# Suffix sums of the stick-breaking heads as two fp32r passes over a high and a low part, in place of one fp32 pass

## The reference

```
z = einsum('bqhd,bshd->bhqs', qb, k) * scale
past = key_pos[None, :] < qpos[:, None]
log_keep = where(past, log_sigmoid(-z), 0.0)
suffix = cumsum(log_keep, axis=3, reverse=True) - log_keep
w = where(past, exp(log_sigmoid(z) + suffix), 0.0)
o = einsum('bhqs,bshd->bqhd', w, v)
```

## Time and profile before

| | |
|---|---|
| median of 3 runs | 1950.08 us |
| lowest, highest | 1949.14, 1953.25 us |
| the profiled execution | 1951.19 us, span 1949.5 us |
| PE busy | 1723.2 us, 88% of the span |
| DVE busy | 1026.1 us, 53% |
| ACT busy | 653.0 us, 33% |
| POOL busy | 591.1 us, 30% |
| stick-breaking stage | about 608 to 730 us of the span |
| DSA stage | about 730 to 780 us of the span |

### The profile page before, as it was taken

The page is one execution under the profiler, slowest core; times in us unless marked ns, Lnnn a source line. Parts: engine busy times, 40 slices in busy tenths (PEclk is TensorE's granted clock), DMA queues, the critical chain, the costliest instruction groups (busy, mean ns, idle before and its releaser), DMA issues.

```text
span 1949.5 us, 23737 instructions
## 1 busy us (share of the span) xinstructions
PE 1723.2 (88%) x9380; PEld 1429.6 (73%) x9385; DVE 1026.1 (53%) x1305; ACT 653.0 (33%) x889; POOL 591.1 (30%) x515
## 2 busy tenths in 40 slices
PE   4997599788787789869999999899987799999997
PEld 3796489568786668748888787677766678888875
DVE  1568567575467675583333324655675743233344
ACT  4312255412122325243232212343444343332222
POOL 0005800262774000467887701222431300000012
PEclk8998799899788889989999999899997999999999
DMA  8553300143532000225565522221110222323221
GB/s 278 164 172 98 119 1 1 34 156 116 165 109 84 25 1 1 65 87 172 182 194 180 168 84 83 84 87 44 65 44 23 65 86 91 102 86 102 94 85 43
DMA packets 152521, 187.14 MB, mean 96 GB/s; under 512 B 6893, under 2 KB 117845, under 8 KB 152436
## 3 DMA queue, kind: packets, MB, share of 16 engines
q1 hardware_dynamic: 152436, 185.96, 29.6%
HBM read 183.85 MB, written 2.10 MB: 95 GB/s over the span
## 4 chain that ended last, share of the span: by engine, by line
PE 58%; POOL 16%; DVE 12%; issue 7%; ACT 4%; DMA 2%; POOLq 0%; SPq 0%; another core or an unknown queue 0%; DVEq 0%; ACTq 0%
PE ps L843 6%; PE ps L844 6%; PE ps L845 6%; POOL msum L627 5%; POOL mraw L620 5%; PE ps L1200 4%; PE ps L1201 4%; PE ps L1202 4%; PE ps L939 2%; PE ps L1234 2%; PE ps L863 2%; PE ps L1236 2%; PE ps L1235 2%; PE ps L865 2%; PE ps L866 2%
## 5 line engine op out<-in xcount | busy, mean ns | idle before, releaser
L1200 PE MATMUL ps<-uH,whi 128*128 128x512 f32 x704 | 278.6, 396 | 25.7 <-DVE uL L1841 25.4
L1202 PE MATMUL ps<-uH,wlo 128*128 128x512 f32 x704 | 276.5, 393 | 0.0
L1201 PE MATMUL ps<-uL,whi 128*128 128x512 f32 x704 | 276.1, 392 | 0.0
L1825 DVE TENSOR_TENSOR wlo<-wraw,whi 128x2048 fp32r<-128x2048 f32 x64 | 157.3, 2458 | 178.6 <-ACT whi L1372 178.4
L620 POOL TENSOR_TENSOR mraw<-mraw,cpad 128x1024 f32<-128x1024 f32 x64 | 129.1, 2017 | 380.8 <-PE ps L782 237.2
L1372 ACT ACTIVATE whi<-wraw 128x2048 fp32r<-128x2048 f32 x71 | 135.7, 1911 | 301.0 <-PE ps L845 268.0
L1200 PEld LDWEIGHTS ps<-uH,whi 128*128 128x128 f32 x704 | 133.7, 190 | 57.0 <-issue 20.8
L2344 DVE TENSOR_TENSOR wlo<-wraw,whi 128x2048 fp32r<-128x2048 f32 x22 | 51.2, 2327 | 206.8 <-ACT whi L1677 206.8
L1202 PEld LDWEIGHTS ps<-uH,wlo 128*128 128x128 f32 x704 | 133.4, 190 | 28.5
L1201 PEld LDWEIGHTS ps<-uL,whi 128*128 128x128 f32 x704 | 133.8, 190 | 27.4
L627 POOL TENSOR_TENSOR msum<-msum,mraw 128x512 f32<-128x512 f32 x96 | 150.8, 1571 | 7.5
(11 more groups left out here) (452 smaller groups left out, 3663.3 us busy)
## 6 DMA issues: line engine op xcount, KB each, us to landing
mraw<-in_w_mod_dram SPq DMA_DIRECT2D x104, 512.0 KB, 3.9
wraw<-in_w_gate_dram SPq DMA_DIRECT2D x22, 1024.0 KB, 5.3
wraw<-in_w_up_dram SPq DMA_DIRECT2D x22, 1024.0 KB, 5.5
wraw<-in_w_down_dram SPq DMA_DIRECT2D x16, 1024.0 KB, 5.0
wraw<-in_w_in_dram SPq DMA_DIRECT2D x11, 1024.0 KB, 5.5
wraw<-in_w_in_even_dram SPq DMA_DIRECT2D x9, 1024.0 KB, 6.6
mfirst<-in_w_mod_dram SPq DMA_DIRECT2D x16, 512.0 KB, 7.2
wraw<-in_w_in_odd_dram SPq DMA_DIRECT2D x16, 512.0 KB, 4.5
```

The lines of the kernel that those rows point to most:

```text
L1200: mm(o, h_, uH[:, k], start=(k == 0), stop=False)
L1201: mm(o, h_, uL[:, k], start=False, stop=False)
L1202: last = mm(o, l_, uH[:, k], start=False, stop=(k == KT - 1))
L1825: V.tensor_tensor(wlo[:, n % 2, :], wraw[:, n % 2, :], whi[:, n % 2, :].bitcast(F32), ALU.subtract).then_inc(lo_done, 1)
```

## The change

A head's softplus `spt` is split: ACT copies it to `spH` as fp32r (`sb_part`), DVE writes the rest `spt - spH` to `spL` as fp32r (`sb_rest`). PE's suffix sums become 10 fp32r matmuls over `spH` and 10 over `spL`, against fp32r copies `rtri` and `rone` of the two constant matrices, which ACT makes once. `spH` lies in the memory of `zw` and `spL` in that of `spt`, so `sb_min(h)` now waits for the suffix sums of head h-2 to be done. One top-k round stands ahead of the first `sb_rest`, and `dsa_max` and `dsa_move` get the width (q+1)*128.

```diff
             def sb_suffix(h):
-                z, s_ = region(h), spt[:, h % 2]
-                pe.wait_ge(sp_rd, h + 1)
-                for kt in range(4):
-                    for k2 in range(kt, 4):
-                        w = SEQ - k2 * P
-                        o0 = ZOFF[kt] + (k2 - kt) * P
-                        last = mm(z[:, o0:o0 + w], negtri[:] if k2 == kt else negone[:], s_[:, ZOFF[k2]:ZOFF[k2] + w],
-                                  start=False, stop=True, skip_group_check=True)
+                z = region(h)
+                if h == 0:
+                    pe.wait_ge(tri_rd, 1)
+                for part in range(2):
+                    s_ = (spH, spL)[part][:, h % 2]
+                    pe.wait_ge((sph_rd, spl_rd)[part], h + 1)
+                    for kt in range(4):
+                        for k2 in range(kt, 4):
+                            w = SEQ - k2 * P
+                            o0 = ZOFF[kt] + (k2 - kt) * P
+                            last = mm(z[:, o0:o0 + w], rtri[:] if k2 == kt else rone[:], s_[:, ZOFF[k2]:ZOFF[k2] + w],
+                                      start=False, stop=(part == 1), skip_group_check=True)
                 last.then_inc(arg_rd, 1)
...
             sb_high(1)
+            act.wait_ge(rp_rd, 1)
+            A(rtri[:], negtri[:], ACT.Copy)
+            A(rone[:], negone[:], ACT.Copy).then_inc(tri_rd, 1)
             split_high(NC1 + 11)
...
+            def sb_part(h):
+                act.wait_ge(sp_rd, h + 1)
+                A(spH[:, h % 2], spt[:, h % 2], ACT.Copy).then_inc(sph_rd, 1)
+
+            sb_part(0)
             for h in range(NH):
                 act.wait_ge(arg_rd, h + 1)
                 A(spt[:, h % 2], region(h), ACT.Exp).then_inc(wgt_rd, 1)
                 if h % 2 == 0 and h + 3 < NH:
                     sb_high(h + 3)
+                if h + 1 < NH:
+                    sb_part(h + 1)
                 if h + 2 < NH:
                     sb_softplus(h + 2)
...
             def sb_min(h):
                 dve.wait_ge(z_rd, h + 1)
                 if h >= 2:
-                    dve.wait_ge(sp_rd, h - 1)
+                    dve.wait_ge(arg_rd, h - 1)
...
+            def sb_rest(h):
+                dve.wait_ge(sph_rd, h + 1)
+                V.tensor_tensor(spL[:, h % 2], spt[:, h % 2], spH[:, h % 2].bitcast(F32), ALU.subtract).then_inc(spl_rd, 1)
...
             sb_max(0)
-            for r_ in range(18, 26):
+            topk(18)
+            sb_rest(0)
+            for r_ in range(19, 26):
                 topk(r_)
...
                 if h in (5, 6):
                     job_low(h + 3, 0, 7, h == 5)
+                if h + 1 < NH:
+                    sb_rest(h + 1)
                 if h >= 1:
                     sb_out(h - 1)
...
             def dsa_max(i):
-                w = (ROWS[i % 4] + 1) * P
+                w = (i % 4 + 1) * P
...
             def dsa_move(i):
-                w = (ROWS[i % 4] + 1) * P
+                w = (i % 4 + 1) * P
```

More of the change, by code:

```diff
@@ L205, in program @@
         jobT, job_hi, job_lo = sem("jobT"), sem("job_hi"), sem("job_lo")
-        z_rd, zmin_rd, zexp_rd, zln_rd, sp_rd, arg_rd, wgt_rd, sv_rd, so_rd = [sem(n) for n in (
-            "z_rd", "zmin_rd", "zexp_rd", "zln_rd", "sp_rd", "arg_rd", "wgt_rd", "sv_rd", "so_rd")]
+        z_rd, zmin_rd, zexp_rd, zln_rd, sp_rd, arg_rd, wgt_rd, sv_rd, so_rd, sph_rd, spl_rd, tri_rd = [sem(n) for n in (
+            "z_rd", "zmin_rd", "zexp_rd", "zln_rd", "sp_rd", "arg_rd", "wgt_rd", "sv_rd", "so_rd", "sph_rd", "spl_rd", "tri_rd")]
         ds_rd, dmx_rd, dp_rd, dt_rd, dpv_rd, do_rd = [sem(n) for n in ("ds_rd", "dmx_rd", "dp_rd", "dt_rd", "dpv_rd", "do_rd")]
@@ L287, in program @@
                                                                      ("ixH", "ixL", "izH", "izL")])[1:]
+        spH, spL = overlay([("spH", [P, 2, 1280], F32R), ("spL", [P, 2, 1280], F32R)])
         zw = s2("zw", [P, 2, 1280])
         spt = s2("spt", [P, 2, 1280])
+        rtri = s2("rtri", [P, P], F32R)
+        rone = s2("rone", [P, P], F32R)
         e2.close()
```

## The result

The changed kernel took 1971.53 us (median of 4 runs, 1968.74 to 1975.88). The kernel before, run beside it, took 1951.66 us (4 runs, 1949.14 to 1955.77). The ratio is 1.0102 with a 95% interval of 1.0075 to 1.0128: slower by 19.9 us, where 11.3 were forecast. The direction was right. The size was not: 1971.53 lies above the range for 8 in 10, 1956.5 to 1968.

What follows compares the result with a forecast made beforehand. The stage was taken to be bound by a chain through PE, DVE and ACT, with PE waiting for DVE's low part. Terms 1.5 + 1.8 + 2.2 + 0 + 3.4 + 1.5 + 0.9 = 11.3 us gave 1961.4 us, 8-in-10 range 1956.5 to 1968.

Steps and rivals of the forecast that it cites:

- step 1: First rest, in DVE's gapless block before low part 3 and scores 2: +1.5 us, range +1.4 to +2.0.
- step 2: Pairs of heads up to scores 6: PE's saving turns into waiting, DVE runs later; first pair +1.8, second +2.2 us.
- step 3: From scores 6 to maximum 7: fuller clock and added rest and half-clock pass cancel, 0 us (-0.3 to +0.6).
- 4, to the last `select`: Head 7: copy and rest now follow maximum 7 and delay DVE's last instructions, +3.4 us.
- 4, to the end of values 7: Head 7: PE idles before the mask, so DSA scores and values run partly at half clock, +1.5 us (0 to 2.5).
- step 5: DSA heads: new widths of maximum and move lengthen the stage by 0.9 us, from +2.0 and -1.2.
- The PE saving: Rival: eight heads each save 1.6 us of PE work, 12.8 in all, about 1938 us; chance 4%.
- the clock: Rival: shorter PE waits lower the clock too, three stretches at 1.2 GHz add 6 or 7 us, 1968; chance 15%.

Runs made afterwards that it cites:

- a_high_pass_only: The changed kernel without the low passes and without DVE's rests, so the sums leave out the low part; 1955.76 us, stage 120.55 us.
- b_copy_and_fp32_pass: The changed kernel with ACT's copies and PE's wait for them, but the old single fp32 suffix and no rests; 1956.10 us, stage 119.06 us.
- d_filler_head_6: The changed kernel with zero-weight matmuls between high and low pass, 8 at heads 2 and 4, 12 at head 6, none at head 7; 1967.03 us.
- b_filler_in_waits: The changed kernel with zero-weight matmuls between high and low pass, 2 at odd heads, 8 at heads 2, 4 and 6; 1965.23 us.
- a_widths_only: The kernel before with only the new (q+1)*128 widths of dsa_max and dsa_move; 1952.24 us, DSA stage 51.64 us.
- a_dve_load_only: The kernel before plus two unused 640-element DVE subtractions at each place of a rest, which nobody waits for; 1961.87 us.

## Why the prediction was right and wrong

| step | forecast | measured in the traces |
|---|---|---|
| 1, scores 0 to scores 2 | +1.5 | +1.95 (25.55 to 27.50) |
| 2, first pair, to scores 4 | +1.8 | +2.15 (27.27 to 29.42) |
| 2, second pair, to scores 6 | +2.2 | +3.5 (24.72 to 28.23) |
| 3, to maximum 7 | 0 | +3.2 (26.09 to 29.26) |
| 4, to the last `select` | +3.4 | +3.3 (10.79 to 14.11) |
| 4, to the end of values 7 | +1.5 | +1.9 (3.54 to 5.46) |
| 5, DSA stage | +0.9 | +2.4 (50.79 to 53.21) |
| sum | 11.3 | 18.4 |

**Right: the prices and the chain.** The rest was priced at 1.42 and took 1.48 (it hands over after 1.40), the copy at 1.27 and took 1.27, a pass at 1.4 at full clock and 2.8 at half, and took 1.44 (677.50 to 678.94) and 2.6 (690.50 to 693.12, where a job follows). The first rest took 1.98 beside POOL, and waited 0.28 us for ACT: the upper end of step 1. By the Trainium skill ("SBUF — State Buffer", section "SBUF: two separate sides") whichever of the two starts first holds the shared ports for its whole instruction, and the other is blocked. The trace agrees. On POOL:

```profile
627.11 1.89 POOL L623 TENSOR_TENSOR mraw<-mraw,cpad 128x1024 f32<-128x1024 f32 x1
629.08 3.76 POOL L630 TENSOR_TENSOR msum<-msum,mraw 128x512 f32<-128x512 f32 x2
```

The rest started at 628.37, 0.63 us ahead of the end of POOL's running addition, and took 0.50 us longer than the others. Then POOL's two sums took 3.76 where they took 2.61. So the rest lost what was left of one POOL instruction. A whole POOL sum of 1.3 us, as the prediction had it, would have made 2.7 and not the upper end of step 1, 2.0.

The PE saving was worth nothing (a_high_pass_only against b_copy_and_fp32_pass), as step 2 had it. Head 7 up to the last `select` came out within 0.1 us, with low part 9 1.9 us later behind maximum 7 (2.0 forecast). The waits for the rest were near what was named: 3.72, 3.80 and 5.24 us at heads 2, 4 and 6 (4 to 5 forecast), 1.55, 0.96 and 1.36 at heads 1, 3 and 5 (1.3 to 2 forecast), and none at head 7. Two slips of the prediction change little: step 5's +2.0 and -1.2 make 0.8 and not 0.9, and what stands behind minimum 4 is result 1, not result 2.

**Wrong: step 3.** It said that after the shorter wait scores 6 might run at full clock, that the half-clock low pass was the whole price of the low clock, and that values 5 follow in full. The first is wrong: scores 6 began at 698.11 with no wait of their own, and still at half, behind half-clock values. The last is the large one: values 5 took 4.47 us, 2.1 more than at full clock (2.39), and because maximum 7 needs them in this stretch they are on the path. Of the +3.2, 2.4 are the wait of maximum 7 for values 5 and 0.8 is the rest in DVE's stream. d_filler_head_6 shows it: with the wait filled the stretch is 26.9, 0.8 above the kernel before, near the walk's upper 0.6.

**Wrong in the same way: step 2's second pair and step 5.** The pair was walked with one low pass at half. Scores 4 were at half from end to end and high pass 3 in part (0.7 us until minimum 5, where 0.2 was forecast), and values 3 at half cost 0.9 (scores 6 start 2.33 us behind low part 7, and 1.44 before). b_filler_in_waits took values 3 back to 2.34, and its pair is 26.81, 1.4 shorter. In step 5 I priced the widths alone. They are 0.85 net; the other 1.6 I put down to a DSA stage entered at half clock behind the 4.02 us wait for the mask. No run changes that wait alone, but all fit: with the new widths the stage is 51.6 to 51.7 us where the wait is at most 0.5 (a_widths_only, b_copy_and_fp32_pass), and 53.2 us or more where it is 2 or more. It is 53.3 us at 0.96 in a_high_pass_only too, which has no low pass; there the wait for the mask is 2.0 us.

**Where the 16 us of the stage come from.** The copies 1.1 (b_copy_and_fp32_pass) and the DVE load about 9 (a_dve_load_only, in proportion) make 10; of the other 6, fillers give back 4.0. About 2 remain for the coupling of low pass, weights and high part that step 2 walked. This account is not exact, since the load run has a low clock of its own (0.80).

**The rival that came true** is the clock, with 15%: "scores and values of some heads run at the 1.2 GHz level", 1968. It had the mechanism and nearly the size. Against it I had held that in the pair shown only the longest waits were followed by a low clock. That was one pair. The kernel before has the counter-example further on: values 5 partly at half (3.05 us for 2.34) behind a wait of 2.46.

```profile
711.20 3.05 PE L1054 MATMUL ps<-T,spt 128*128 128x64 f32 x20 [2.46 <-DVE T L2170]
```

The clock in the same stage was 0.83 before any change. A change that adds a wait to nearly every pass moves that number, and the likeliest case should have carried it.

## What to carry to other kernels

In this stage, where PE waits for DVE, moving work from PE to DVE and ACT lost twice: about three quarters of the load on DVE counted, and the freed PE time turned into waits that halved the clock of what followed. Price the low clock on all that follows a wait, here up to 12 us of PE work, and not on the first pass behind it alone. Look at all waits in the whole stage before you decide which of them count; here waits of 1.5 to 2.5 us had half-clock work behind them. Put a new DVE instruction ahead of one that waits for another engine, not behind it: that alone gave back 7 of the 16 us here.

## What the runs showed of the hardware that I had not expected

- The level can fall with a delay. Behind a wait of 1.72 us the next pass ran at full clock and the values behind it at half (4.47 us for 2.39, in b_filler_in_waits); behind 1.48 us, with one of 0.61 us two microseconds before it, values were at half from the start (4.46, in a_dve_load_only).
- It can stay low with no idle time at all: low pass 4, a job, values 3 and scores 6 of the kernel after ran at a granted clock of 0.50 from 690.50 to 702.40, with PE busy for all 11.90 us.
- PE's busy time hides this: 92.40 us in the stage before and 92.06 after, though the work after is some 13 us less at full clock.
- A subtraction of 1280 fp32 from SBUF took 1.48 us alone and 1.98 beside POOL, and POOL's two sums behind it took 3.76 us in place of 2.61.
